# Queries and keys of the differential attention computed by features, their rotary rows exchanged by small transfers

## The reference, cut to what matters

```
DA_HEADS = 8
DA_HEAD_DIM = D_MODEL // (2 * DA_HEADS)      # 64
DA_ROT = DA_HEAD_DIM // 4                    # 16

def apply_rope(x, cos, sin):
    ...
    x1, x2 = jnp.split(x, 2, axis=-1)
    return jnp.concatenate([x1 * c - x2 * s, x2 * c + x1 * s], axis=-1)

def diff_attention(h, w_qkv, lq1, lk1, lq2, lk2, subln_g, w_o, lambda_init, cos, sin):
    qkv = h @ w_qkv
    q, k, v = jnp.split(qkv, 3, axis=-1)
    q = q.reshape(b, s, DA_HEADS, 2, DA_HEAD_DIM)
    k = k.reshape(b, s, DA_HEADS, 2, DA_HEAD_DIM)
    v = v.reshape(b, s, DA_HEADS, 2 * DA_HEAD_DIM)
    q = jnp.concatenate([apply_rope(q[..., :DA_ROT], cos, sin), q[..., DA_ROT:]], axis=-1)
    k = jnp.concatenate([apply_rope(k[..., :DA_ROT], cos, sin), k[..., DA_ROT:]], axis=-1)
    ...
        sc = jnp.einsum('bqhcd,bkhcd->bhcqk', qb, k).astype(jnp.float32) * scale
        p = masked_softmax(sc, chunk_mask(blk, s)[None, None, None])
        a = p[:, :, 0] - lam * p[:, :, 1]
        return jnp.einsum('bhqk,bkhe->bqhe', a.astype(v.dtype), v)
    ...
    o = rms_norm(o, subln_g) * (1.0 - lambda_init)
    return o.reshape(b, s, D_MODEL) @ w_o
```

## Time and profile before

| what | before |
|---|---|
| median of 3 runs | 1745.36 us |
| the profiled execution, its own time | 1745.7 us |
| span of that execution, first to last instruction | 1743.9 us |
| granted TensorE clock | 0.998 of full |
| PE busy | 1728.2 us, 99% of the span |
| DVE busy | 1091.1 us, 63% |
| ACT busy | 785.4 us, 45% |
| GpSimd busy | 134.5 us, 8% |
| chain that ended last | PE 94%, DVE 3%, ACT 1%, issue 1%, DMA 1% |

### The profile page before, as it was taken

The page is one execution under the profiler, slowest core; times in us unless marked ns, Lnnn a source line. Parts: engine busy times, 40 slices in busy tenths (PEclk is TensorE's granted clock), DMA queues, the critical chain, the costliest instruction groups (busy, mean ns, idle before and its releaser), DMA issues.

```text
span 1743.9 us, 22594 instructions
## 1 busy us (share of the span) xinstructions
PE 1728.2 (99%) x8782; PEld 1460.0 (84%) x8782; DVE 1091.1 (63%) x1719; ACT 785.4 (45%) x1398; POOL 134.5 (8%) x138
## 2 busy tenths in 40 slices
PE   9999999999999999999999999999999999999998
PEld 7888888888888888888888888889898888888887
DVE  5788644344346666685864764665888676376375
ACT  5553532222235555544532432456876454244244
POOL 2003200000005100002000000022101200000000
PEclk9999999999999999999999999999999999999999
DMA  5212333333333221122333333323111233333341
GB/s 169 73 51 85 93 97 97 97 97 97 97 97 97 78 69 61 61 73 85 96 97 97 97 93 101 97 76 103 39 49 37 81 92 98 98 98 97 98 127 61
DMA packets 128355, 152.78 MB, mean 88 GB/s; under 512 B 9286, under 2 KB 101992, under 8 KB 128248
## 3 DMA queue, kind: packets, MB, share of 16 engines
q1 hardware_dynamic: 128088, 151.26, 28.3%
q10 hardware_dynamic: 160, 0.07, 0.0%
HBM read 148.61 MB, written 2.10 MB: 86 GB/s over the span
## 4 chain that ended last, share of the span: by engine, by line
PE 94%; DVE 3%; ACT 1%; issue 1%; DMA 1%; POOL 0%; ACTq 0%; DVEq 0%; POOLq 0%
PE bk L1908 24%; PE bk L1909 23%; PE bk L1910 23%; PE bk L1937 5%; PE bk L1939 4%; PE bk L1938 4%; PE bk L1913 4%; PE bk L2035 2%; PE bk L2069 1%; PE bk L2068 1%; PE bk L1996 1%; PE bk L2023 1%; DVE WL L2100 1%; PE bk L2025 0%; PE bk L2024 0%
## 5 line engine op out<-in xcount | busy, mean ns | idle before, releaser
L1908 PE MATMUL bk<-R,WH 128*128 128x512 f32 x1844 | 724.0, 393 | 1.8 <-DVE R L2106 1.6
L1910 PE MATMUL bk<-R,WL 128*128 128x512 f32 x1844 | 718.4, 390 | 0.0
L1909 PE MATMUL bk<-R,WH 128*128 128x512 f32 x1844 | 718.1, 389 | 0.0
L2100 DVE TENSOR_TENSOR WL<-RAW,WH 128x1024 fp32r<-128x1024 f32 (+4 forms) x278 | 343.7, 1237 | 483.2 <-ACT WH L2302 482.2
L2302 ACT ACTIVATE WH<-RAW 128x1024 fp32r<-128x1024 f32 (+4 forms) x278 | 288.0, 1036 | 604.3 <-PE bk L1910 546.6
L1908 PEld LDWEIGHTS bk<-R,WH 128*128 128x128 f32 x1844 | 346.8, 188 | 73.4 <-issue 2.2
L1910 PEld LDWEIGHTS bk<-R,WL 128*128 128x128 f32 x1844 | 346.4, 188 | 72.8
L1909 PEld LDWEIGHTS bk<-R,WH 128*128 128x128 f32 x1844 | 346.8, 188 | 68.9
L1937 PE MATMUL bk<-WH,R 128*128 128x256 f32 (+4 forms) x432 | 146.0, 338 | 0.3 <-DVE KT L2106 0.3
L1939 PE MATMUL bk<-WL,R 128*128 128x256 f32 (+4 forms) x432 | 140.7, 326 | 0.0
L1938 PE MATMUL bk<-WH,R 128*128 128x256 f32 (+4 forms) x432 | 140.5, 325 | 0.0
(11 more groups left out here) (170 smaller groups left out, 1503.6 us busy)
## 6 DMA issues: line engine op xcount, KB each, us to landing
RAW<-in_ffn_w_up_dram SPq DMA_DIRECT2D x176, 256.0 KB, 3.0
RAW<-in_ffn_w_down_dram SPq DMA_DIRECT2D x44, 512.0 KB, 3.7
RAW<-in_w_gate_dram SPq DMA_DIRECT2D x44, 256.0 KB, 2.8
RAW<-in_w_up_dram SPq DMA_DIRECT2D x44, 256.0 KB, 3.1
RAW<-in_w_down_dram SPq DMA_DIRECT2D x22, 512.0 KB, 3.7
RAW<-in_da_w_qkv_dram SPq DMA_DIRECT2D x32, 256.0 KB, 2.9
RAW<-in_w_out_dram SPq DMA_DIRECT2D x8, 512.0 KB, 3.6
RAW<-in_da_w_qkv_dram SPq DMA_DIRECT2D x8, 512.0 KB, 3.6
```

Source lines behind the costliest of these rows:

```text
L1908: e.matmul(dst, lh, rh, start=start, stop=False)
L1909: e.matmul(dst, lh, rl, start=False, stop=False)
L1910: return e.matmul(dst, ll, rh, start=False, stop=stop)
L2100: e.tensor_tensor(low, sides(st.n, RAW[:, r, 0:m]), high.bitcast(F32), ALU.subtract).then_inc(on["wlo_dve"], 1)
```

## The change

- Queries and keys come by gemm_f (features by tokens), with the same weights and the same number of matmuls. The steps tok_qk, rope (in this attention), heads and the small step eighth go. The latent attention keeps its own.
- Each of a group's four banks (m = 0, 1 queries, m = 2, 3 keys) goes through ev_rotated: ACT copies it plain to SBUF (rot_copy); DVE multiplies the bank by a table of cosines (scaled); SP issues four transfers, SBUF to SBUF, each of 8 rows by 512, which exchange the rotary rows into a tile that is otherwise zero (rot_swap); GpSimd multiplies that by the table of sines and adds it to the scaled tile (rot_mix, two instructions 128 by 512); ACT and DVE split the sum.
- The two tables (1 in the rows that don't turn) come from memory once (rot_load) and are multiplied once by the norm's factor, spread by one more "over" on PE and two DVE instructions (rot_spread). Two memsets clear the exchanged tiles.
- There are two plain, two exchanged and four result tiles for all groups, in the space of the token buffers. The latent attention's first copies into it wait for all four groups.
- The planner is told 3.2 us for a rot_mix, and that the exchanged rows land 2.5 us after the copy. The wait for the exchanged tile's last reader is in the steps, but not in that 2.5 us.

```
+    if kind == "rot_mix":
+        return 3200.0
...
+        rot = Group()
+        rot.spread, rot.cos, rot.sin, rot.swaps = None, flat(1)[:, 0:S], flat(1)[:, S:2 * S], [0, 0]
+        rot.out, rot.first_swapped, rot.swapped, rot.plain = Ring(4), 4, Ring(2), Ring(2)
+        for n, x in enumerate(rot.swapped.fr):
+            x.i = rot.first_swapped + n
+        for n, x in enumerate(rot.plain.fr):
+            x.i = 6 + n
+        rot.at = lambda x: flat(0)[:, x.i * S:x.i * S + S] if x.i < 5 else flat(1)[:, (x.i - 3) * S:(x.i - 2) * S]
+
+        def taken_from(ring):
+            while not ring.fr:
+                yield None
+            return ring.get()
+
+        def rotation(N):
+            emit("rot_load", after=[])
+            landing(s_rot, free_at["pe"] + 20000.0)
+            for x in rot.swapped.fr:
+                st = yield step("rot_zero", dst=rot.at(x), after=counts(tok_free))
+                x.free = [st.pool]
+            while N() is None or N().rooted is None:
+                yield None
+            b = yield from bank()
+            st = yield step("over", bank=b.i, r=N().r, after=counts([b.free, N().rooted]))
+            st = yield step("rot_spread", bank=b.i, after=[st.pe, (s_rot, 16)])
+            put_bank(b, st.dve)
+            rot.spread = st.dve
...
-            def ev_qk(t, bk, done):
-                free = tok_free if g < 2 else before.ups
-                while N.rooted is None or len(free) < 4:
-                    yield None
-                st = yield step("tok_qk", tok=g % 2, t=t, bank=bk.i, rq=N.r8[:, t:t + 1], rk=N.r[:, t:t + 1],
-                                after=counts([done, free, N.rooted]))
-                G.toks.append(st.act)
-                put_bank(bk, st.act)
-
-            def turn_in():
-                while len(G.toks) < 4 or not flags.consts:
-                    yield None
-                tok = TOKS[g % 2]
-                v = tok[:, :, 0:512].rearrange("p t (h c) -> p t h c", c=64)
-                cs, sn = (CN[:, o:o + 32].rearrange("p (t c) -> p t c", c=8).unsqueeze(2).to_broadcast([P, 4, 8, 8])
-                          for o in (C_CDA, C_SDA))
-                t1, t2 = (tok[:, :, o:o + 64].rearrange("p t (h c) -> p t h c", c=8) for o in (512, 576))
-                st = yield step("rope", v1=v[:, :, :, 0:8], v2=v[:, :, :, 8:16], cs=cs, sn=sn, t1=t1, t2=t2, after=counts(G.toks))
-                G.cut = [st.pool]
-                for n in (0, 1):
-                    spawn(turn_q(n))
-                for n in (0, 1):
-                    spawn(turn_k(n))
-
-            def turn_q(n):
-                while G.Q[n].h is None:
-                    yield None
-                yield from turn_heads(g % 2, 0, P, n, G.cut, G.ups, q_tiles(P, G.Q))
+            def ev_rotated(m, bk, done):
+                while rot.spread is None or m < 2 and G.Q[m].h is None:
+                    yield None
+                y, z, o = (yield from taken_from(rot.plain)), (yield from taken_from(rot.swapped)), (yield from taken_from(rot.out))
+                st = yield step("rot_copy", dst=rot.at(y), bank=bk.i, after=counts([done, y.free]))
+                copied = st.act
+                st = yield step("scaled", dst=rot.at(o), bank=bk.i, bc=rot.cos, after=counts([copied, o.free, rot.spread]))
+                put_bank(bk, st.dve)
+                which = z.i - rot.first_swapped
+                rot.swaps[which] += 64
+                landed_in = (s_swap[which], rot.swaps[which])
+                emit("rot_swap", src=rot.at(y), dst=rot.at(z), which=which, after=counts([copied, z.free]))
+                ready_at[id(landed_in[0]), landed_in[1]] = at_time(copied) + 2500.0
+                rot.plain.put(y, landed_in)
+                st = yield step("rot_mix", z=rot.at(z), o=rot.at(o), after=[landed_in, st.dve, rot.spread])
+                rot.swapped.put(z, st.pool)
+                if m < 2:
+                    lo = yield from split_pair(G.Q[m], rot.at(o), [st.pool], 0.125)
+                else:
+                    while before and not before.valued:
+                        yield None
+                    i = G.kbase + 4 * (m - 2)
+                    lo = yield from halves(KT[:, i, :], KT[:, i + 1, :], rot.at(o), [st.pool], None, [kfree[i + x] for x in range(4)])
+                    kready[i] = [lo]
+                rot.out.put(o, lo)
+                G.ups.append(lo)
                 G.split += 1
                 G.turned = G.split == 4
 
-            def turn_k(n):
-                while before and not before.valued:
-                    yield None
-                yield from turn_heads(g % 2, 256, P, n, G.cut, G.ups, k_pair(G.kbase))
-                G.split += 1
-                G.turned = G.split == 4
-
-            if kind == "fg":
-                yield from gemm_f(N.X, 8, 4, ev_turned)
-            else:
-                spawn(turn_in())
-                yield from gemm_t(N.X, 8, 512, ev_qk)
+            yield from gemm_f(N.X, 8, 4, ev_turned if kind == "fg" else ev_rotated)
...
-                while NM.rooted is None or len(Gs[2].ups) < 4:
+                while NM.rooted is None or any(len(G.ups) < 4 for G in Gs):
...
+                elif st.kind == "rot_swap":
+                    for done in st.after:
+                        w.wait_ge(*done)
+                    for r in (0, 64):
+                        e.dma_start(st.dst[r:r + 8, :], st.src[r + 8:r + 16, :]).then_inc(s_swap[st.which], 16)
+                        e.dma_start(st.dst[r + 8:r + 16, :], st.src[r:r + 8, :]).then_inc(s_swap[st.which], 16)
...
+                elif k == "rot_spread":
+                    for done in st.after:
+                        w.wait_ge(*done)
+                    e.tensor_tensor(rot.cos, BK[st.bank][:, :], rot.cos, ALU.mult).then_inc(on["rot_spread_dve"], 1)
+                    e.tensor_tensor(rot.sin, BK[st.bank][:, :], rot.sin, ALU.mult).then_inc(on["rot_spread_dve"], 1)
...
-                elif k == "tok_qk":
-                    for done in st.after:
-                        w.wait_ge(*done)
-                    e.activation(TOKS[st.tok][:, st.t, 0:256], BK[st.bank][:, 0:256], ACT.Copy, scale=st.rq)
-                    e.activation(TOKS[st.tok][:, st.t, 256:512], BK[st.bank][:, 256:512], ACT.Copy, scale=st.rk).then_inc(on["tok_qk_act"], 1)
+                elif k == "rot_copy":
+                    for done in st.after:
+                        w.wait_ge(*done)
+                    e.activation(st.dst, BK[st.bank][:, :], ACT.Copy).then_inc(on["rot_copy_act"], 1)
...
+                elif k == "rot_mix":
+                    for done in st.after:
+                        w.wait_ge(*done)
+                    e.tensor_tensor(st.z, st.z, rot.sin, ALU.mult).then_inc(on["rot_mix_pool"], 1)
+                    w.wait_ge(on["rot_mix_pool"], st.pool0 + 1)
+                    e.tensor_tensor(st.o, st.o, st.z, ALU.add).then_inc(on["rot_mix_pool"], 1)
...
```

79 lines of the change are left out of this document (40 added, 39 removed).

## The result

The changed kernel takes 1754.95 us (median of 4 runs, 1754.36 to 1755.52) against 1745.69 for the kernel before in the same comparison: a ratio of 1.0054, 95% interval 1.0042 to 1.0067. It is 9.3 us slower, where 1744.0 was predicted with a range up to 1752.

The account below looks back on a forecast made before the run. PE, busy 99% of the span, was taken to bound the kernel. 6.6 us less PE work, minus 2.4, 1.5 and 1.3 of new waits, left 1.4 gained: 1744.0 us, range 1738.5 to 1752.

Parts of the forecast that it names:

- The exchange, 3.7 us after its copy: SP's four transfers per tile: 1.1 us of issuing plus 2.6 to land, 3.7 us after the copy (2.5 to 6.6).
- the case of late weights: A weight load on SP stands behind an exchange that waits for a mix; 1748.8 us, chance 0.04.
- The price of late mixes, +2.4 (0 to 15): Queries and keys 1.4 us later than planned; 0.8 us of PE idle in each of groups 1 to 3.
- PE's work, -6.6: Four runs of 16 transposes go, 7.0 us; one added "over" costs 0.36; net 6.6 us less PE work.
- The values, +1.5 (0.3 to 4): PE's values have one step of cover left after block 3's turn; three places at 0.5 us of waiting.
- the three places named: The places where the values keep only one step of cover, each taken at 0.5 us.
- GpSimd beside DVE, +1.3 (0 to 10): GpSimd's work slows DVE instructions; 0.4 us of PE idle per group of the last three, rounded up to 1.3.
- The third case: GpSimd shuts out DVE's instructions with two SBUF operands: 13 us over three groups, 1751.8 us, chance 0.22.
- the sign that I had set: PE waits over 10 us in 560 to 800 us, two-operand DVE instructions at twice their length, show GpSimd shutting out DVE.

Follow-up runs that it names:

- the moved line: Changed kernel with each exchange written out right behind its copy, not behind DVE's multiplication; same instructions: 1747.14 us, ratio 1.0013.
- the kernel with the short mix and the moved line: Changed kernel with exchanges written out right behind their copies and GpSimd's mix cut to 8 columns: 1742.16 us, ratio 0.9981.
- the short mix: Changed kernel in its own order, with transfers, GpSimd's two mix instructions cut from 512 to 8 columns: 1741.85 us, ratio 0.9982.
- the memsets: Changed kernel in its own order, each mix replaced by 8 columns plus four memsets of 512, signal last: 1750.63 us, ratio 1.0029.

## Why the prediction was wrong

- **The exchange, 3.7 us after its copy.** This step failed. The transfer itself takes 4.0, near enough. But I let it start with the copy. SP works in order, and in group 0 the exchange stood 7 us behind a load that waited for DVE; in the last group an exchange that was free to go stood behind one that waited for a mix. I had asked what a waiting exchange does to the loads (the case of late weights, 0.04; WH and WL released no wait of PE in this stage) and not what a waiting load, or another exchange, does to the exchange.
- **The price of late mixes, +2.4 (0 to 15).** It follows from the start of the exchange. Measured: 7.8 us for the queue's order (the moved line) and 2.4 for the mixes' length, 10.2. The mechanism was the predicted one (splits on ACT ahead of an exp, PE waiting for p_two), but one place took most of it, where I had laid 0.8 us on each of three groups. Group 0 stood at nothing, and PE waits 1.2 us there for its first key tile. The 10.2 are inside the term's bounds. The range should have held those bounds; it didn't, since I closed it at 1752.
- **The clock.** No term stood for it. 3.4 us were lost at half clock behind the 4.8 us wait. They are within the 7.8, since both go together.
- **PE's work, -6.6.** The 60 matmuls went, but the term was too large. In the kernel with the short mix and the moved line, whose PE hardly idles, PE is busy in the stage for 4.9 us less than before (269.9 us in the row above):

```profile
557.80:825.80 268.00, 265.07 (x1622) 225.19 (x1621) 193.32 (x402) 139.21 (x311) 27.79 (x44) 1.00 0.26 77
```

- **The values, +1.5 (0.3 to 4).** Near: 2.0 us of waits on PT remain with short mixes, 1.6 of them at one block, group 2's second head, which is one of the three places named.
- **GpSimd beside DVE, +1.3 (0 to 10).** 2.6 us, undersized by half. The third case (13 us by some 10 instructions a group) was wrong in its price: 11.7 us of slowing on DVE are 2.6 on PE. By the sign that I had set (over 10 us of waits, DVE at twice its length) the waits pointed to this case, but the lengths didn't: a low part of weights took 1506 ns from 590 to 641 us, against 1222.
- **Sum.** -4.9 + 10.2 + 2.0 + 2.6 = +9.9; measured +9.3. This split holds for one path only, the one that puts SP's queue in order first. The parts overlap: with the queue left as it was, the memsets are worth 4.3 us and the short mix a further 8.8, and then the order of the queue is worth nothing (1741.85 and 1742.16). A late exchange and a long mix cost what they do together.

## What to carry to other kernels

Before a small transfer is put into a chain, read its queue's order: what each entry ahead of it waits for, and whether one that is free to go stands behind one that isn't. Put the transfer out directly behind its producer, and keep its consumer off any engine on which others stand behind it. Then look at the granted clock behind each new wait: what it costs comes on top, and it differs from execution to execution.
